# In the SSD scan of a two-block transformer kernel, GpSimd's row masks and the halving of the weight slabs change places

## The chip, the cores and the metric

The kernel runs on one core of one Trainium2 chip. The metric is device microseconds of one execution. Three runs of the kernel before gave 1665.68, 1666.03 and 1666.28 us, so the median is 1666.03 us.

## The reference, cut to what matters

The reference computes two residual blocks over 512 tokens of width 1024. The change lies in the second block's SSD mixer, a scan with 32 heads of 64 channels in 4 groups. For one head the reference computes, chunk by chunk,

```
a_cum    = cumsum(dt * A)
decay_in = exp(where(causal, a_cum[l] - a_cum[s], -inf))
y        = (C B^T * decay_in) (x * dt)           (+ the state carried from earlier chunks)
y        = (y + x * d_skip) * silu(z)
y        = rms_norm over each of the 4 groups of 512 channels
```

The kernel doesn't carry a state. It forms the whole causal 512 x 512 matrix of each head, of which 1280 columns per partition are kept (the causal blocks of 128 x 128), so the decay is one masked exponential of 128 x 1280 and the scan is one product of that matrix with the head's inputs.

## The kernel before, in words

Weights come as slabs of 1 MB (128 x 2048 f32). A slab is loaded by SyncE into one of three slots (`raw`). Then ScalarE writes its high half (`weight_head`, tile `w_hi`, line 458) and VectorE writes the rest (`weight_tail`, tile `w_lo`, line 994, `raw` minus `w_hi`). TensorE multiplies with both halves in three products (lines 1835 to 1837). `w_lo` has the same place as `raw`.

The stage of the change runs over 16 pairs of heads. Beside the pairs, TensorE makes the 16 tiles of z, two from each of 8 slabs. The slabs of the gates follow. Five engines work in a pipeline. Each engine runs its own list of instructions in order, and semaphores join the lists. I call one turn of the loop over `pair` a body, and name the instructions so:

- TensorE, body p: the tile z(p+1), then `pair_values(p)`, line 2292, which I call values(p). It needs both weighted rows of pair p and bank 6, which gated(p-1) sets free. After values(2), values(6) and values(10) the scores of the next group follow, line 2260.
- SyncE: `sum_row(hd)` loads the 128 x 1280 row of head hd from DRAM (line 387) into one of five buffers `p2`. The row of head hd may start when values((hd-5)//2) has ended.
- GpSimd: mask(hd) is `row_masked(hd)`, two affine selects of 128 x 256, lines 1788 and 1789. Body p runs mask(2p+4), product(p) (line 1799, y times the gate, which waits for gated(p)), mask(2p+5), square(p) (line 1802), and, except where p is a multiple of four, sum(p) (line 1805).
- ScalarE, body p: the tanh of z(p), then exp(2p+2) and exp(2p+3), four activations each, which wait for mask(2p+2) and mask(2p+3). Where p is odd, a `weight_head` follows.
- VectorE, body p: gated(p-1) (line 1456, which waits for values(p-1)), gate(p) (line 1450), where p is even and not zero a `weight_tail`, where p is 3, 7 or 11 the copies of a group's scores (line 1467), then weighted(2p+2) and weighted(2p+3) (line 1476), which wait for exp(2p+2) and exp(2p+3).

So gated(p) in VectorE's body p+1 releases product(p) on GpSimd, and weighted(2p+5) stands in that same body p+1, ahead of gated(p+1) in body p+2.

Of the kernel before, what the change touches and what calls it, by code (L numbers as in the profile page):

```python
# [28 lines left out]
SSD_H, SSD_P, SSD_G, XS_T, BC_T, TAPS = 32, 64, 4, 16, 8, 4  # L29
# [29 lines left out]
SLAB0, SLABS, FREED, PLACE, _freed, _freed_wide = {}, {}, {}, [], 0, 2  # L59
# [24 lines left out]
def build(nc, x_d, slabs_d, ada_d, cols_d, gate_w_d, pool_w_d, consts_d, inv_d, rope_d, qkg_d, out_d):  # L84
# [159 lines left out]
    def sem(name):  # L244
        if name not in sems:
            sems[name] = nc.alloc_semaphore(name)
        return sems[name]
# [29 lines left out]
    def paired(back):  # L277
        out, used = [], 0
        for j in (1, 0, 2, 3) if back else (0, 1, 3, 2):
            lo, hi = (0, P * (j + 1)) if back else (P * j, S)  # L280
            out.append((j, lo, hi, used))
            used += hi - lo
        return out
# [4 lines left out]
    def diagonals(a, back):  # L288

        first, wide = (P, a[:, 2 * P:]) if back else (7 * P, a[:, 0:8 * P])  # L290
        wide = wide.rearrange("p (r c) -> p r c", r=2)
        near = a[:, first:first + 2 * P].rearrange("p (r c) -> p r c", r=2)
        far = wide[:, :, 3 * P:] if back else wide[:, :, 0:P]
        return far, near
# [7 lines left out]
    def group_total(g):  # L302
        return xbc[:, XS_T + g, :]

    def group_square(pair):
        return xbc[:, XS_T + (SSD_G if pair % 4 else 0) + pair // 4, :]
# [62 lines left out]
    def width(n):  # L369
        return UQ_COLS if n in UQ_AT else SLAB  # L370

    block = nc.Block()
    with block:
# [79 lines left out]
        def _(act):  # L453
# [3 lines left out]
            def fn(out, in_, f, **kw):  # L457
                return act.activation(out, in_, f, **kw)  # L458
# [8 lines left out]
            def weight_head(n):  # L467

                act.wait_ge(sem(f"raw_in{n % SLOTS}"), 16 * (n // SLOTS) + 16)
                if n >= SLOTS:  # L470

                    act.wait_ge(sem("tile_done"), 2 * (n - SLOTS) + 2)
                do.tell(fn(w_hi[:, n % SLOTS, 0:width(n)], raw[:, n % SLOTS, 0:width(n)], ACT.Copy), "w_head", n + 1)
# [323 lines left out]
            def half_tanh(pair):  # L797
                act.wait_ge(sem("tile_done"), 2 * SLAB0["z"] + pair + 1)
                if pair >= 2:

                    act.wait_ge(sem("z_used"), pair - 1)
                do.tell(fn(zt[pair % 2][:], z_banks[pair % 2][:], ACT.Tanh, scale=0.5), "z_tanh", pair + 1)

            def exponentials(hd):
                act.wait_ge(sem("row_masked"), hd + 1)
                e2, shift = p2[hd % len(p2)], nac_col[:, :, hd:hd + 1]
                for j, lo, hi, used in paired(0):
                    row = e2[:, used:used + hi - lo]
                    ins = fn(row, row, ACT.Exp, bias=shift[:, j, :])
                    if j != TOK - 2:  # L810
                        do(ins)
                    else:
                        do.tell(ins, "e2_made", hd + 1)
# [3 lines left out]
            for pair in range(XS_T):  # L817
                half_tanh(pair)
                if pair + 1 < XS_T:
                    for hd in (2 * pair + 2, 2 * pair + 3):  # L820
                        exponentials(hd)
                if pair % 2:
                    weight_head(SLAB0["z"] + pair // 2 + 2)

            def group_root(g):
                act.wait_ge(sem("group_mean"), g + 1)
                do.tell(fn(rs_g[:, g, :], group_banks[g][:], ACT.Sqrt, bias=eps), "group_root", g + 1)
# [103 lines left out]
            for step in range(QH + 1):  # L931
                if step < QH:
                    hd = step
# [8 lines left out]
                if step:  # L942
                    hd = step - 1
# [39 lines left out]
        def _(dve):  # L983
# [6 lines left out]
            def weight_tail(n):  # L990

                dve.wait_ge(sem("w_head"), n + 1)
                part = slice(0, width(n))
                do.tell(dve.tensor_tensor(w_lo[:, n % SLOTS, part], raw[:, n % SLOTS, part], w_hi[:, n % SLOTS, part].bitcast(f32),  # L994
                                          ALU.subtract), "w_split", n + 1)
# [452 lines left out]
            def gate(pair):  # L1448
                dve.wait_ge(sem("z_tanh"), pair + 1)
                free(dve.scalar_tensor_tensor(zt[pair % 2][:], zt[pair % 2][:], 1.0, z_banks[pair % 2][:], ALU.add, ALU.mult), "z", pair)  # L1450

            def gated_pair(pair):

                y = xbc[:, pair, :]
                dve.wait_ge(sem("pv2_done"), TOK * (pair + 1))
                do.tell(dve.scalar_tensor_tensor(y, y, col("d_skip", pair), banks[6][:], ALU.mult, ALU.add), "ys_made", pair + 1)
# [5 lines left out]
            def scores_copied(g):  # L1462

                for j, lo, hi, used in sorted(paired(0), key=lambda block_row: block_row[0] != 2):
                    bank, first = score_place(j)
                    dve.wait_ge(sem("s2_done"), 2 * g + (1 if j == 2 else 2))
                    ins = dve.tensor_copy(sm[:, used:used + hi - lo], banks[bank][:, first:first + hi - lo])
                    if j >= 2:
                        do.tell(ins, "s2_taken", 2 * g + j - 1)
                    else:  # L1470
                        do(ins)

            def weighted_scores(hd):
                e2 = p2[hd % len(p2)]
                dve.wait_ge(sem("e2_made"), hd + 1)
                do.tell(dve.tensor_tensor(e2[:], e2[:], sm[:], ALU.mult), "p2_made", hd + 1)  # L1476
# [6 lines left out]
            for pair in range(XS_T):  # L1483
                if pair:
                    gated_pair(pair - 1)
                gate(pair)
                if pair % 2 == 0 and pair:
                    weight_tail(SLAB0["z"] + pair // 2 + 1)
                if pair % 4 == 3 and pair + 1 < XS_T:
                    scores_copied(pair // 4 + 1)  # L1490
                if pair + 1 < XS_T:
                    weighted_scores(2 * pair + 2)
                    weighted_scores(2 * pair + 3)
            gated_pair(XS_T - 1)
            weight_tail(SLAB0["gates"] + 1)
            dve.wait_ge(sem("z_used"), XS_T)
            for g in range(SSD_G):
                if g == SSD_G - 1:
# [229 lines left out]
        def _(pool):  # L1728
# [55 lines left out]
            def row_masked(hd):  # L1784

                pool.wait_ge(sem(f"row_in{hd % len(p2)}"), 16 * (hd // len(p2)) + 16)
                wide, near = diagonals(p2[hd % len(p2)], 0)
                do(pool.affine_select(wide, wide, [[0, 2], [1, P]], ALU.is_ge, never, base=0, channel_multiplier=-1))  # L1788
                do.tell(pool.affine_select(near, near, [[0, 2], [1, P]], ALU.is_ge, never, base=0, channel_multiplier=-1),  # L1789
                        "row_masked", hd + 1)  # L1790

            for hd in range(4):
                row_masked(hd)
            for pair in range(XS_T):
                if pair + 2 < XS_T:
                    row_masked(2 * pair + 4)

                pool.wait_ge(sem("ys_made"), pair + 1)
                do.tell(pool.tensor_tensor(xbc[:, pair, :], zt[pair % 2][:], xbc[:, pair, :], ALU.mult), "z_used", pair + 1)  # L1799
                if pair + 2 < XS_T:  # L1800
                    row_masked(2 * pair + 5)
                do(pool.tensor_tensor(group_square(pair), xbc[:, pair, :], xbc[:, pair, :], ALU.mult))
                if pair % 4:
                    total = group_total(pair // 4)
                    do.tell(pool.tensor_tensor(total, total, group_square(pair), ALU.add), "square_added", pair - pair // 4)

            for n in range(8, 16):
                pool.wait_ge(sem("key_scale"), n - 7)
# [6 lines left out]
            for hd in range(QH):  # L1815
# [5 lines left out]
                if hd >= 3 and hd % 2:  # L1821
                    pair = (hd - 3) // 2
# [797 lines left out]
```

## Time and profile before

| | |
|---|---|
| median of three runs | 1666.03 us |
| profiled execution: its own time, its span | 1667.77 us, 1666.0 us |
| TensorE busy with matmuls in the span | 98% (1635.8 us) |
| VectorE, ScalarE, GpSimd busy | 66%, 44%, 16% |
| mean granted TensorE clock | 0.999 |
| product (line 1799), 16 times | 1.284 us median, 3.226 us longest |
| ScalarE waiting for GpSimd's masks, 783 to 925 us | 38.9 us in 18 waits |
| VectorE waiting for ScalarE's exponentials, 783 to 925 us | 31.3 us in 13 waits |

Times in the tables and rows are microseconds from the span's start unless marked ns. Busy time counts the instruction from its start to its end, so an instruction that has been started and is held back counts as busy too. TensorE's matmuls are pipelined and their ends are modelled.

### The profile page before, as it was taken

What the parts mean: (1) busy time and instruction counts of PE and PEld (TensorE: products, weight loads), DVE (VectorE), ACT (ScalarE), POOL (GpSimd) and SP (SyncE); (2) the same over time, 40 slices, a digit from 0 to 9 for tenths busy, and PEclk for the clock granted to TensorE, in tenths of its full rate; (3) what the DMA queues carried; (4) which work ended last, traced back from release to release, by engine and by line L of the source; (5) the groups of instructions that cost most, each with busy time, mean ns of one, the idle gap of its engine ahead of it and who ended that gap; (6) DMA issues with size and microseconds to landing.
All of it is one profiled execution on the core that took longest, in us unless ns stands there. A gap on an engine that the chain in (4) does not pass through costs nothing.

```text
span 1666.0 us, 20328 instructions
## 1 busy us (share of the span) xinstructions
PE 1635.8 (98%) x7871; PEld 1313.4 (79%) x7871; DVE 1098.8 (66%) x1378; ACT 736.6 (44%) x971; POOL 258.5 (16%) x243
## 2 busy tenths in 40 slices
PE   6999999999999999999999999999999999999999
PEld 3888778888898887887666788886688888888887
DVE  2888878544575576877777865548868886642464
ACT  3443334222374236546676433538822454531241
POOL 0005100050220000001899200004600000000000
PEclk9999999999999999999999999999999999999999
DMA  9544322222222232225555222220032222222222
GB/s 386 200 186 177 142 77 101 83 95 102 101 102 101 99 129 82 100 78 201 196 204 182 76 101 74 95 101 26 2 114 89 101 102 101 86 91 101 101 101 101
DMA packets 30224, 195.33 MB, mean 117 GB/s; under 512 B 3376, under 2 KB 3856, under 8 KB 9904
## 3 DMA queue, kind: packets, MB, share of 16 engines
q1 hardware_dynamic: 26240, 167.66, 27.9%
q10 hardware_dynamic: 3888, 26.38, 4.0%
q8 instruction: 62, 1.02, 0.2%
q14 instruction: 34, 0.28, 0.1%
HBM read 189.66 MB, written 4.36 MB: 116 GB/s over the span
## 4 chain that ended last, share of the span: by engine, by line
PE 82%; DVE 7%; ACT 4%; POOL 4%; issue 1%; DMA 1%; ACTq 0%; SPq 0%; DVEq 0%; POOLq 0%
PE bank L1835 25%; PE bank L1837 24%; PE bank L1836 24%; DVE p L1476 2%; ACT p L458 2%; POOL p L1788 1%; PE bank L2408 1%; PE bank L2434 1%; PE bank L2420 1%; DMA x<-x_in 1%; POOL p L1789 1%; DVE w_lo L994 1%; PE bank L2125 1%; PE bank L2107 1%; POOL xbc L1799 1%
## 5 line engine op out<-in xcount | busy, mean ns | idle before, releaser
L1835 PE MATMUL bank<-h,w_hi 128*128 128x512 f32 (+1 forms) x1152 | 451.0, 392 | 3.7 <-DVE w_lo L994 3.0
L1836 PE MATMUL bank<-h,w_hi 128*128 128x512 f32 (+1 forms) x1152 | 445.1, 386 | 0.0
L1837 PE MATMUL bank<-h,w_lo 128*128 128x512 f32 (+1 forms) x1152 | 445.0, 386 | 0.0
L458 ACT ACTIVATE w_hi<-raw 128x2048 fp32r<-128x2048 f32 (+1 forms) x133 | 247.4, 1860 | 310.7 <-DMA raw<-slabs 301.6
L994 DVE TENSOR_TENSOR w_lo<-raw,w_hi 128x2048 fp32r<-128x2048 f32 (+1 forms) x125 | 291.5, 2332 | 98.2 <-ACT w_hi L458 94.8
L1835 PEld LDWEIGHTS bank<-h,w_hi 128*128 128x128 f32 x1152 | 216.4, 188 | 53.4 <-issue 5.6
L1837 PEld LDWEIGHTS bank<-h,w_lo 128*128 128x128 f32 x1152 | 216.4, 188 | 44.3
L1836 PEld LDWEIGHTS bank<-h,w_hi 128*128 128x128 f32 x1152 | 216.5, 188 | 43.7 <-issue 1.4
L1835 PE MATMUL bank<-a_hi,w_hi 128*128 128x512 f32 x432 | 168.3, 390 | 0.6 <-DVE a_lo L998 0.3
L1837 PE MATMUL bank<-a_hi,w_lo 128*128 128x512 f32 x432 | 168.1, 389 | 0.0
L1836 PE MATMUL bank<-a_lo,w_hi 128*128 128x512 f32 x432 | 168.1, 389 | 0.0
L1835 PEld LDWEIGHTS bank<-a_hi,w_hi 128*128 128x128 f32 x432 | 81.1, 188 | 18.0 <-DVE a_lo L998 0.7
L1836 PEld LDWEIGHTS bank<-a_lo,w_hi 128*128 128x128 f32 x432 | 81.1, 188 | 16.9
L1837 PEld LDWEIGHTS bank<-a_hi,w_lo 128*128 128x128 f32 x432 | 81.1, 188 | 16.9
L458 ACT ACTIVATE p<-p,nac_col 128x512 f32<-128x512 f32 (+3 forms) x128 | 72.1, 563 | 42.8 <-POOL p L1789 38.9
L1708 DVE SCALAR_TENSOR_TENSOR facc<-fpad,cols,facc 128x512 f32<-128x512 f32 x88 | 66.2, 752 | 32.6 <-ACT facc L458 30.2
L1088 DVE SCALAR_TENSOR_TENSOR x<-bank,mod,x 128x512 f32<-128x512 f32 x24 | 18.0, 751 | 99.0 <-PE bank L1837 98.9
L1476 DVE TENSOR_TENSOR p<-p,sm 128x1280 f32<-128x1280 f32 x32 | 56.0, 1749 | 32.3 <-ACT p L458 31.3
L1431 DVE SCALAR_TENSOR_TENSOR cacc<-cpad,cols,cacc 128x512 f32<-128x512 f32 x72 | 54.4, 755 | 29.2 <-ACT cacc L458 27.1
L1788 POOL TENSOR_SCALAR_AFFINE_SELECT p<-p 128x256 f32<-128x256 f32 x32 | 43.7, 1365 | 160.0 <-DMA p<-sum_rows 157.9
L1086 DVE TENSOR_TENSOR x<-bank,x 128x512 f32<-128x512 f32 x16 | 11.1, 692 | 69.4 <-PE bank L1837 69.4
L1835 PE MATMUL bank<-ys_hi,w_hi 128*128 128x512 f32 x128 | 50.6, 395 | 0.0
(403 smaller groups left out, 2523.4 us busy)
## 6 DMA issues: line engine op xcount, KB each, us to landing
raw<-slabs SPq DMA_DIRECT2D x127, 1024.0 KB, 4.8
ada_chunk<-ada ACTq DMA_DIRECT2D x24, 1024.0 KB, 7.0
p<-sum_rows SPq DMA_DIRECT2D x32, 640.0 KB, 5.5
x<-x_in SPq DMA_DIRECT2D x4, 1024.0 KB, 9.3
spill_x<-x SPq DMA_DIRECT2D x1, 2048.0 KB, 10.6
x<-spill_x SPq DMA_DIRECT2D x2, 1024.0 KB, 6.0
out<-x SPq DMA_DIRECT2D x8, 256.0 KB, 2.0
raw<-slabs SPq DMA_DIRECT2D x2, 768.0 KB, 4.2
```

Of the source, the lines that this page charges most:

```text
L458: return act.activation(out, in_, f, **kw)
L994: do.tell(dve.tensor_tensor(w_lo[:, n % SLOTS, part], raw[:, n % SLOTS, part], w_hi[:, n % SLOTS, part].bitcast(f32), ALU.subtract), "w_sp ...
L1088: ins = dve.scalar_tensor_tensor(x[:, m, :], bank[:], mod[:, gate + m:gate + m + 1], x[:, m, :], ALU.mult, ALU.add)
L1431: ins = dve.scalar_tensor_tensor(acc, pad[:, tap:tap + S], col("conv_w", TAPS * n + tap), acc, ALU.mult, ALU.add)
L1476: do.tell(dve.tensor_tensor(e2[:], e2[:], sm[:], ALU.mult), "p2_made", hd + 1)
L1708: ins = dve.scalar_tensor_tensor(acc, pad[:, tap:tap + S], col("convf_w", TAPS_F * tile + tap), acc, ALU.mult, ALU.add)
L1788: do(pool.affine_select(wide, wide, [[0, 2], [1, P]], ALU.is_ge, never, base=0, channel_multiplier=-1))
L1789: do.tell(pool.affine_select(near, near, [[0, 2], [1, P]], ALU.is_ge, never, base=0, channel_multiplier=-1), "row_masked", hd + 1)
L1799: do.tell(pool.tensor_tensor(xbc[:, pair, :], zt[pair % 2][:], xbc[:, pair, :], ALU.mult), "z_used", pair + 1)
L1835: pe.matmul(out, w[0], a[0], start=start, stop=False)
L1836: pe.matmul(out, w[0], a[1], start=False, stop=False)
L1837: return pe.matmul(out, w[1], a[0], start=False, stop=stop)
```

## The change

Three engines' lists change their order. No instruction is added or taken away, and no shape changes. On ScalarE the `weight_head` of a slab moves from the end of an odd body to the middle of the even body in front of it, between the two exponentials. On VectorE the `weight_tail` moves from the start of an even body to the middle of the odd body in front of it, between the two weighted rows. On GpSimd mask(2p+5) moves from between product and square to behind square and sum. The following mask(2p+6), which stood right behind the sum as the first of the next body, stays behind it.

```diff
             for pair in range(XS_T):
                 half_tanh(pair)
                 if pair + 1 < XS_T:
-                    for hd in (2 * pair + 2, 2 * pair + 3):
-                        exponentials(hd)
-                if pair % 2:
+                    exponentials(2 * pair + 2)
+                if pair % 2 == 0:
                     weight_head(SLAB0["z"] + pair // 2 + 2)
+                if pair + 1 < XS_T:
+                    exponentials(2 * pair + 3)
```

```diff
                 if pair:
                     gated_pair(pair - 1)
                 gate(pair)
-                if pair % 2 == 0 and pair:
-                    weight_tail(SLAB0["z"] + pair // 2 + 1)
                 if pair % 4 == 3 and pair + 1 < XS_T:
                     scores_copied(pair // 4 + 1)
                 if pair + 1 < XS_T:
                     weighted_scores(2 * pair + 2)
+                if pair % 2:
+                    weight_tail(SLAB0["z"] + pair // 2 + 2)
+                if pair + 1 < XS_T:
                     weighted_scores(2 * pair + 3)
             gated_pair(XS_T - 1)
-            weight_tail(SLAB0["gates"] + 1)
```

```diff
-            for hd in range(4):
+            for hd in range(5):
                 row_masked(hd)
             for pair in range(XS_T):
-                if pair + 2 < XS_T:
-                    row_masked(2 * pair + 4)
 
                 pool.wait_ge(sem("ys_made"), pair + 1)
                 do.tell(pool.tensor_tensor(xbc[:, pair, :], zt[pair % 2][:], xbc[:, pair, :], ALU.mult), "z_used", pair + 1)
-                if pair + 2 < XS_T:
-                    row_masked(2 * pair + 5)
                 do(pool.tensor_tensor(group_square(pair), xbc[:, pair, :], xbc[:, pair, :], ALU.mult))
                 if pair % 4:
                     total = group_total(pair // 4)
                     do.tell(pool.tensor_tensor(total, total, group_square(pair), ALU.add), "square_added", pair - pair // 4)
+                for hd in (2 * pair + 5, 2 * pair + 6):
+                    if hd < SSD_H:
+                        row_masked(hd)
```

## Rows read from the trace of the kernel before

**Rows 1.** One window of four bodies; columns: length, each engine's busy us, clock, DMA.
```profile
855.00:891.00 36.00, 34.25 (x172) 23.22 (x170) 27.59 (x23) 24.31 (x39) 33.08 (x28) 1.00 0.58 205
```
**Rows 2.** Waits of TensorE from 783 to 925 us: total, times, longest.
```profile
PE bank L2292 <- DVE xbc L1456: 4.2, 4, 1.1
PE bank L1835 <- DVE w_lo L994: 2.8, 4, 0.9
```
**Rows 3.** The chain that ended last, in order of time: start, us, what.
```profile
841.08 0.73 ACT p L458
...
848.66 2.01 DVE p L1476
850.75 2.44 DVE p L1476
```
**Rows 4.** Timeline of VectorE: start, us, line, operation, idle before and its releaser.
```profile
846.56 2.07 DVE L1467 COPY sm<-bank 128x256 f32<-128x256 f32 x4
...
853.22 0.75 DVE L1456 SCALAR_TENSOR_TENSOR xbc<-xbc,cols,bank 128x512 f32<-128x512 f32 x1
854.00 0.69 DVE L1450 SCALAR_TENSOR_TENSOR zt<-zt,bank 128x512 f32<-128x512 f32 x1
854.72 2.82 DVE L994 TENSOR_TENSOR w_lo<-raw,w_hi 128x2048 fp32r<-128x2048 f32 x1
857.58 1.57 DVE L1476 TENSOR_TENSOR p<-p,sm 128x1280 f32<-128x1280 f32 x1
861.97 1.49 DVE L1476 TENSOR_TENSOR p<-p,sm 128x1280 f32<-128x1280 f32 x1 [2.82 <-ACT p L458]
...
932.36 2.29 DVE L994 TENSOR_TENSOR w_lo<-raw,w_hi 128x2048 fp32r<-128x2048 f32 x1
```
**Rows 5.** Timeline of GpSimd over the same body.
```profile
849.41 2.42 POOL L1805 TENSOR_TENSOR xbc<-xbc 128x512 f32<-128x512 f32 x1
...
854.11 1.28 POOL L1799 TENSOR_TENSOR xbc<-zt,xbc 128x512 f32<-128x512 f32 x1 [0.19 <-DVE xbc L1456]
855.47 2.34 POOL L1788 TENSOR_SCALAR_AFFINE_SELECT p<-p 128x256 f32<-128x256 f32 x1
857.88 1.54 POOL L1789 TENSOR_SCALAR_AFFINE_SELECT p<-p 128x256 f32<-128x256 f32 x1
859.50 1.04 POOL L1802 TENSOR_TENSOR xbc<-xbc 128x512 f32<-128x512 f32 x1
860.62 1.29 POOL L1805 TENSOR_TENSOR xbc<-xbc 128x512 f32<-128x512 f32 x1
...
863.79 0.41 POOL L1789 TENSOR_SCALAR_AFFINE_SELECT p<-p 128x256 f32<-128x256 f32 x1
```
**Rows 6.** Timeline of ScalarE: the first body, then the body shown above.
```profile
784.09 4.73 ACT L458 ACTIVATE p<-p,nac_col 128x512 f32<-128x512 f32 x8 [1.35 <-POOL p L1789]
...
859.51 2.35 ACT L458 ACTIVATE p<-p,nac_col 128x512 f32<-128x512 f32 x4 [3.15 <-POOL p L1789]
861.90 0.60 ACT L458 ACTIVATE zt<-bank 128x512 f32<-128x512 f32 x1
...
869.11 1.93 ACT L458 ACTIVATE w_hi<-raw 128x2048 fp32r<-128x2048 f32 x1
```
**Rows 7.** Timeline of VectorE: gated(0) and gated(14).
```profile
790.45 0.75 DVE L1456 SCALAR_TENSOR_TENSOR xbc<-xbc,cols,bank 128x512 f32<-128x512 f32 x1
...
917.00 0.75 DVE L1456 SCALAR_TENSOR_TENSOR xbc<-xbc,cols,bank 128x512 f32<-128x512 f32 x1
```
**Rows 8.** Timeline of TensorE: one values(p).
```profile
864.39 2.37 PE L2292 MATMUL bank<-p,xdt 128*64 128x512 f32 x16 [1.02 <-DVE xbc L1456]
```
**Rows 9.** DMAs of the tile sum_rows, 36 issues: us from issue to landing.
```profile
DMA to landing us min/median/max: 3.7/5.4/7.7
```
**Rows 10.** Two windows around the one fall of TensorE's clock near 1142 us.
```profile
1136.00:1138.00 2.00, 0.88 (x8) 0.91 (x9) 1.36 (x6) 1.92 (x4) 1.33 (x3) 1.00 0.89 373
...
1143.00:1144.00 1.00, 1.00 (x2) 0.23 (x1) 0.68 (x2) 0.71 (x3) 0.91 (x2) 0.50 0.00 0
```

## The prediction

> **What bounds the kernel now.** I read the window sums first. TensorE is busy 98% of the span, but over four bodies of the SSD loop, 36.00 us, it is busy 34.25 us while GpSimd counts 33.08 [rows 1]. The waits of TensorE come next: in the loop it stands 4.2 us for gated(p) and 2.8 us for `w_lo` [rows 2], 7.0 us in all. The chain in order of time then shows whose chain it is: it runs through GpSimd's mask, ScalarE's exponential, VectorE's weighted rows and gated(p) [rows 3], and comes back to GpSimd.
>
> The timelines give the cycle. gated(7) starts at 853.22, product(7) at 854.11, and mask(19) is through at 859.42. The exponential starts at 859.51, weighted(19) at 861.97, and gated(8) at 863.49 (861.97 + 1.49 + 0.03) [rows 4 to 6]. Body 8 thus takes 10.27 us. From gated(0) to gated(14) there are 14 bodies in 917.00 - 790.45 = 126.55 us [rows 7], 9.04 each. TensorE alone needs about 33 to 34 us for four. So the stage has two bounds close to each other, and a longer cycle shows in the time at once.
>
> **What one port does.** Two engines hold each other back. The `weight_tail` issued at 854.72 takes 2.82 us where one alone takes 2.29 [rows 4]: it begins its work at 857.54 - 2.29 = 855.25, 0.14 before product(7) ends (855.39). A weighted row takes 1.49 alone and 2.44 behind a sum that ends at 851.83: again it begins 0.14 to 0.15 before that end [rows 3, 5]. The other way round, the sum issued at 849.41 ends 1.16 after the weighted row in front (850.67), its own 1.29 less 0.13. A select of 0.41 ends 0.27 after the VectorE instruction that it met: 857.81 behind the tail's 857.54, and 859.42 behind the weighted row's 859.15 [rows 4, 5]. gated and gate keep 0.75 and 0.69 beside GpSimd's work, so these two are taken as free of it.
>
> The Trainium skill, "SBUF — State Buffer", section "SBUF: two separate sides", describes this as an exclusive lock on a shared port pair: a VectorE instruction with two SBUF inputs and a GpSimd instruction take turns, and the loser blocks fully. The trace agrees (2.82 against 2.29). By the page the sum comes out as it does below; with no lock it would be 1671 in place of 1701.
>
> **Part 1: mask(2p+5) behind square and sum.** This is the step that costs. It stands on the cycle gated(p), product(p), mask(2p+5), exp(2p+5), weighted(2p+5), gated(p+1). The change puts square(p), 1.04, and sum(p), 1.29, each with a gap of 0.07 to 0.08, between product and mask, onto the cycle. mask(2p+6) is needed one body later and doesn't gain anything that was missing.
>
> I work out one body from the start of gated (0.00), all with the durations above.
> - Without any lock: product 0.89 to 2.18, square 2.25 to 3.29, sum 3.37 to 4.66, two selects to 5.62, exponential 5.71 to 8.07, weighted row 8.18 to 9.67, gated 9.70. Without a sum 8.33. Both are lower bounds of a body.
> - With the lock, even bodies (sum, no tail). exp(2p+2) is early: exp(2p+1) ended 0.11 before weighted(2p+1), that is at -1.63, and a tanh of 0.60, an exponential of 2.35 and gaps bring it to 1.39 [rows 6]. So weighted(2p+2) is issued at 1.50, held by product to 2.03, ends 3.52. Square, issued 2.25, ends at 3.52 + 0.91 = 4.43, sum at 5.79, the selects at 6.28 and 6.76. Exponential 6.85 to 9.21, weighted 9.32 to 10.81, gated at 10.84.
> - Bodies 1, 5, 9, 13 (no sum, but the moved tail). As above to square 4.43. The tail is issued at 3.55, held by square to 4.28, ends 6.57. The first select waits for it: 6.85. The second 7.33. Exponential 7.42 to 9.78, weighted 9.89 to 11.38, gated at 11.41.
> - Bodies 3, 7, 11 (copies, sum and tail). The copies take 1.50 to 3.57 [rows 4] and let square (3.29) pass. Sum 3.37 to 4.66 holds the weighted row, which ends at 6.00; the first select ends 6.28. The tail, issued 6.03, runs to 8.42; the second select ends 8.69. Exponential 8.78 to 11.14, weighted to 12.74, gated at 12.77.
>
> The 14 bodies are 7 x 10.84 + 4 x 11.41 + 3 x 12.77 = 75.9 + 45.6 + 38.3 = 159.8 us, against 126.55: **+33.3 us**.
>
> **Part 2: ScalarE's half earlier.** `weight_head` takes 1.93 [rows 6]. In body 0 the masks are long made and exp(2), exp(3) follow each other without a gap (4.73 for eight activations), so the head delays exp(3), weighted(3) and gated(0) by 1.93 + 0.03: **+1.95 us**. From body 2 on exp(2p+2) ends at 1.39 and mask(2p+3) at 6.76, so the head ends at 3.35 and is hidden by the wait for GpSimd; were that cover gone, it would cost 1.95 in every even body.
>
> **Part 3: VectorE's rest earlier.** TensorE needs the slab two bodies later, so its 2.8 us of waits for `w_lo` go. They buy nothing: TensorE's next wait, for gated, grows instead. The cost of the tail on the cycle is in part 1. After the loop one tail of 2.3 us less stands in VectorE's list, beside 16 tiles of gates that keep TensorE busy; I take 0.
>
> **Rows and slabs.** No DMA is added. Row 2p+5 starts when values(p) ends and lands in 5.4, at most 7.7 us [rows 9]. values(p) starts once gated(p-1) has ended, 0.87 after its start, takes 2.37 [rows 8], and the next gated(p) is 11 us after gated(p-1). So the row lands at most 3.24 + 7.7 = 10.9 after gated(p-1), about when gated(p) starts, and its mask is not due for 4.5 us more. SyncE's order of rows and slabs stays, and a slab waits for z tiles that TensorE ends earlier in its list than the values a row waits for. 0.
>
> **Sum.** +33.3 + 1.95 = +35.2 us. The profiled execution took 1667.77 for a span of 1666.0, so the span would be 1701.2 and its own time 1703.0. On the median of the runs, 1.7 lower: 1666.0 + 35.2 = **1701.2 us**.
>
> **The rivals.**
> - *The lock costs less than it seems.* Square then hides behind the weighted row, or the select gets in ahead of the tail. Without tails on the cycle: 4 x 9.45 + 10 x 10.84 = 146.2, +19.6 + 1.95, 1687.6 us. With no lock at all: 4 x 8.33 + 10 x 9.70 = 130.3, +3.8 + 1.95, 1671.7 us. For it: the lock's length after a select is read from two rows. Against: it repeats in every pair of instructions shown. 15%, nearly all of it at the upper price.
> - *TensorE's clock falls in the wider gaps.* TensorE has about 8 us of work in a body of 11.4, so it stands 3.5 us in each. Near 1142 the clock was at its lower level, 1.2 GHz (0.50), after TensorE had stood still and then run matmuls with breaks; at 1136 to 1138, with 0.88 us busy of 2.00, it was still 1.00 [rows 10]. A body wholly at 1.2 GHz is 2 x 7.9 = 15.8 us, so it decides only where most of a body runs so; a short fall costs less than the 3.5 us that TensorE waits. With half of the 14 bodies at the lower level: 7 x (15.8 - 11.4) = +31 more, 1732 us; with three of them, 1714. 8%. The Trainium skill, "TensorE: Matmul & The Clock Gate", section "What's actually happening", says that an idle TensorE is put to half its clock. No run here shows such gaps repeated.
> - *The other side: TensorE is the bound afterwards.* Its two waits of 7.0 us go and the time is 1666.0 - 7.0 = 1659 us. It needs the cycle to be under 8.5 us, so mask(2p+5) must be off it: GpSimd would have to take it while product or square waits. For it: GpSimd's selects lose up to 1.93 us each to the tail in bodies of 10.27, and the tail moves. Against: its list is in order, and the cycle without any lock is already 9.70. It decides once GpSimd's part, 5.62 us from gated to the last select without any lock, falls under 4.4. 3%, with results down to no change put here.
>
> **How the numbers follow.** Forecast 74%, less lock 15%, clock 8%, other side 3%. The forecast's own spread is some 4 us either way (0.3 us in each of 14 bodies). The range reaches to the first rival's upper price and the smaller clock case: 1686 to 1714. A difference of 0.2% is 3.3 us, about what can be told from no change: faster 2%, same 2%, slower 96%.
>
> **What would show it.** Right: in GpSimd's timeline the selects follow the sum; from gated to gated 10.8, 11.4 and 12.8 us in that pattern; no wait for `w_lo`, 30 to 40 us of TensorE's waits for gated; ScalarE's waits for masks near 5 us in even bodies; weighted rows of 2.0 us beside product. Gated(0) comes 2 us late. Wrong: selects of 0.41 throughout (no lock), a granted clock below 0.95 in the loop, GpSimd waiting for rows, or bodies under 9 us.

## The result and the profile after

The changed kernel takes 1701.13 us, the median of 4 runs (1700.54 to 1702.94), against 1665.86 us of the kernel before. The ratio is 1.0214, with a 95% interval of 1.0196 to 1.0231. It is slower by 35.3 us; 35.2 us were forecast. The profiled execution took 1702.94 us for a span of 1701.2 us. Its line numbers are shifted: gated is L1457, gate L1451, a weighted row L1477, a `weight_tail` L995, product L1798, square L1799, sum L1802, the two selects of a mask L1789 and L1790.

First the waits from 783 to 962 us (total, times, longest), one line each for TensorE, VectorE, ScalarE and GpSimd:

```profile
PE bank L2292 <- DVE xbc L1457: 31.0, 11, 4.7
...
DVE p L1477 <- ACT p L458: 65.4, 16, 5.8
...
ACT p L458 <- POOL p L1790: 70.7, 14, 7.4
...
POOL xbc L1798 <- DVE xbc L1457: 63.8, 15, 6.6
```

The wait for `w_lo` is gone, as the change means it to be, and TensorE's wait for gated has grown from 4.2 to 31.0 us [rows 2]. VectorE, ScalarE and GpSimd wait for each other in a ring: GpSimd for gated, ScalarE for the mask, VectorE for the exponential. TensorE stands outside and waits for the ring. No engine is the bound; the way round is.

The timeline of VectorE shows bodies 7, 8 and 9, from gated to gated:

```profile
859.45 0.75 DVE L1457 SCALAR_TENSOR_TENSOR xbc<-xbc,cols,bank 128x512 f32<-128x512 f32 x1
860.23 0.69 DVE L1451 SCALAR_TENSOR_TENSOR zt<-zt,bank 128x512 f32<-128x512 f32 x1
860.95 2.07 DVE L1468 COPY sm<-bank 128x256 f32<-128x256 f32 x4
863.06 2.40 DVE L1477 TENSOR_TENSOR p<-p,sm 128x1280 f32<-128x1280 f32 x1
865.49 2.38 DVE L995 TENSOR_TENSOR w_lo<-raw,w_hi 128x2048 fp32r<-128x2048 f32 x1
870.67 1.49 DVE L1477 TENSOR_TENSOR p<-p,sm 128x1280 f32<-128x1280 f32 x1 [2.80 <-ACT p L458]
872.20 0.75 DVE L1457 SCALAR_TENSOR_TENSOR xbc<-xbc,cols,bank 128x512 f32<-128x512 f32 x1
...
873.70 2.02 DVE L1477 TENSOR_TENSOR p<-p,sm 128x1280 f32<-128x1280 f32 x1
881.47 1.49 DVE L1477 TENSOR_TENSOR p<-p,sm 128x1280 f32<-128x1280 f32 x1 [5.75 <-ACT p L458]
883.00 0.75 DVE L1457 SCALAR_TENSOR_TENSOR xbc<-xbc,cols,bank 128x512 f32<-128x512 f32 x1
...
886.55 3.02 DVE L995 TENSOR_TENSOR w_lo<-raw,w_hi 128x2048 fp32r<-128x2048 f32 x1
892.85 1.49 DVE L1477 TENSOR_TENSOR p<-p,sm 128x1280 f32<-128x1280 f32 x1 [3.28 <-ACT p L458]
894.38 0.75 DVE L1457 SCALAR_TENSOR_TENSOR xbc<-xbc,cols,bank 128x512 f32<-128x512 f32 x1
```

They take 12.75, 10.80 and 11.38 us; 12.77, 10.84 and 11.41 were worked out. Body 8 of before took 10.27 [rows 4]. The timeline of GpSimd in body 8 shows the new order on the way:

```profile
873.10 1.27 POOL L1798 TENSOR_TENSOR xbc<-zt,xbc 128x512 f32<-128x512 f32 x1 [4.01 <-DVE xbc L1457]
874.45 2.17 POOL L1799 TENSOR_TENSOR xbc<-xbc 128x512 f32<-128x512 f32 x1
876.69 1.27 POOL L1802 TENSOR_TENSOR xbc<-xbc 128x512 f32<-128x512 f32 x1
878.04 0.41 POOL L1789 TENSOR_SCALAR_AFFINE_SELECT p<-p 128x256 f32<-128x256 f32 x1
878.52 0.41 POOL L1790 TENSOR_SCALAR_AFFINE_SELECT p<-p 128x256 f32<-128x256 f32 x1
```

Square takes 2.17 in place of 1.04 because it met the weighted row of 873.70, and that row takes 2.02 in place of 1.49 because it met product. Between product and mask there are now 3.7 us (878.04 - 874.37) where there was a gap of 0.08 [rows 5]. ScalarE's exponential starts at 879.02, right behind the select of 878.52.

### The profile page after: what moved, and what is told of

Its sections match the earlier page's. It is cut to its first block, busy times and chain, and to the rows that moved or that the text cites. A ratio compares the mean times of both kernels' runs of the same rounds, so it can differ in the third digit from the quotient of the medians.

```text
span 1701.2 us, 20328 instructions
## 1 busy us (share of the span) xinstructions
PE 1647.2 (97%) x7871; PEld 1319.4 (78%) x7871; DVE 1099.5 (65%) x1378; ACT 736.1 (43%) x971; POOL 243.0 (14%) x243
## 4 chain that ended last, share of the span: by engine, by line
PE 81%; DVE 6%; POOL 5%; ACT 5%; issue 1%; DMA 1%; ACTq 0%; SPq 0%; POOLq 0%; DVEq 0%
PE bank L1835 24%; PE bank L1837 24%; PE bank L1836 24%; ACT p L458 3%; PE bank L2408 2%; POOL xbc L1799 2%; DVE p L1477 1%; PE bank L2434 1%; PE bank L2420 1%; POOL xbc L1798 1%; POOL p L1789 1%; DMA x<-x_in 1%; DVE w_lo L995 1%; PE bank L2125 1%; PE bank L2107 1%
## 5 line engine op out<-in xcount | busy, mean ns | idle before, releaser
L995 DVE TENSOR_TENSOR w_lo<-raw,w_hi 128x2048 fp32r<-128x2048 f32 (+1 forms) x125 | 292.2, 2337 | 100.5 <-ACT w_hi L458 97.1
L1477 DVE TENSOR_TENSOR p<-p,sm 128x1280 f32<-128x1280 f32 x32 | 56.0, 1749 | 66.3 <-ACT p L458 65.4
L2292 PE MATMUL bank<-p,xdt 128*64 128x512 f32 (+3 forms) x256 | 46.7, 516 | 31.0 <-DVE xbc L1457 31.0
L2292 PEld LDWEIGHTS bank<-p,xdt 128*64 128x64 f32 x256 | 20.5, 159 | 54.9 <-DVE p L1477 35.4
```

The lines of the kernel that those rows point to most:

```text
L2292: last = pe.matmul(banks[6][64 * half:64 * half + 64, lo:hi], xdt[:, j, SSD_P * hd:SSD_P * hd + SSD_P], p2[hd % len(p2)][:, used:used + hi ...
```

## The experiments

Each experiment is compared with runs of the kernel before on the same chip (median 1666.43 us for the first four, 1666.23 us for the last two). Its line numbers can differ by a few from those above, so the rows are told apart by their operations and tiles.

**e1_masks_only.** GpSimd's part alone.

```diff
-            for hd in range(4):
+            for hd in range(5):
                 row_masked(hd)
             for pair in range(XS_T):
-                if pair + 2 < XS_T:
-                    row_masked(2 * pair + 4)
...
-                if pair + 2 < XS_T:
-                    row_masked(2 * pair + 5)
...
+                for hd in (2 * pair + 5, 2 * pair + 6):
+                    if hd < SSD_H:
+                        row_masked(hd)
```

> GpSimd's part of the change alone; ScalarE's and VectorE's lists stay as before. Theory A (mask(2p+5) behind square and sum stands on the cycle gated, product, mask, exponential, weighted row, gated): the tail now stands at the start of the even bodies, so the bodies take about 12.8, 10.8, 12.8 and 9.5 us in place of 10.8, 12.8, 10.8 and 11.4, and their sum is the same as with the whole change: +33 us, 1699 us. Theory B (the slab halves in the middle of the bodies cost the time, GpSimd's order is harmless): no more than 2 us over the kernel before, 1668 us.

Measured: 1701.26 us, ratio 1.0209 (1.0194 to 1.0224). The bodies from gated(4) on take 9.44, 12.76, 10.84 and 12.74 us, and the 14 bodies 159.6 us, against 159.4 with the whole change. The next rows are VectorE's timeline of this kernel in body 5, with no tail in it (gated 835.99 to 845.43):

```profile
835.99 0.75 DVE L1456 SCALAR_TENSOR_TENSOR xbc<-xbc,cols,bank 128x512 f32<-128x512 f32 x1
...
843.91 1.49 DVE L1476 TENSOR_TENSOR p<-p,sm 128x1280 f32<-128x1280 f32 x1 [4.41 <-ACT p L458]
845.43 0.75 DVE L1456 SCALAR_TENSOR_TENSOR xbc<-xbc,cols,bank 128x512 f32<-128x512 f32 x1
```

So the order of GpSimd's list costs the whole 35 us by itself (1701.26 - 1666.43 = 34.8). Where the tail stands changes which body is long, and not the sum. Theory B falls.

**e2_halves_only.** ScalarE's and VectorE's part alone, GpSimd as before.

```diff
+                    exponentials(2 * pair + 2)
+                if pair % 2 == 0:
                     weight_head(SLAB0["z"] + pair // 2 + 2)
+                if pair + 1 < XS_T:
+                    exponentials(2 * pair + 3)
...
                     weighted_scores(2 * pair + 2)
+                if pair % 2:
+                    weight_tail(SLAB0["z"] + pair // 2 + 2)
+                if pair + 1 < XS_T:
                     weighted_scores(2 * pair + 3)
```

> ScalarE's and VectorE's part alone; GpSimd's list stays as before. Theory A: weighted(2p+3) now stands behind a tail, and the tail meets GpSimd's second mask in odd bodies; bodies of about 10.3, 8.4, 10.6 and 8.7 us, so +5 to +6 us, 1671 to 1672 us, and TensorE's waits for w_lo are gone. Theory B: +33 us, 1699 us. A third theory, that the earlier halves are good in themselves and only GpSimd's part spoils them: 1666 less TensorE's 2.8 us of waits for w_lo, 1663 us.

Measured: 1671.85 us, ratio 1.0030 (1.0019 to 1.0041), +5.4 us. The bodies from gated(2) on take 10.57, 8.63, 9.18 and 8.62 us. Its waits of TensorE in the loop:

```profile
PE bank L2293 <- DVE xbc L1457: 10.5, 11, 1.9
```

The 2.8 us for `w_lo` are gone, and the waits for gated grow by more than that, from 4.2 to 10.5 us. The earlier halves lose by themselves too, so the third theory falls with theory B. Beside the masks' move they cost nothing that can be measured, since 1701.13 and 1701.26 us are the same: the costs of two edits on one ring don't add.

**e3_masks_first.** The kernel before, with the mask moved the other way.

```diff
                 if pair + 2 < XS_T:
                     row_masked(2 * pair + 4)
+                    row_masked(2 * pair + 5)
...
-                if pair + 2 < XS_T:
-                    row_masked(2 * pair + 5)
                 do(pool.tensor_tensor(group_square(pair), xbc[:, pair, :], xbc[:, pair, :], ALU.mult))
```

> The kernel before, but GpSimd takes mask(2p+5) before product(p), right behind mask(2p+4); the halves stay as before. Theory A: the mask leaves the cycle through product(p); it then waits only for its row, which may start when values(p) has ended and lands 5 to 8 us later. With 5.5 us to land the bodies average 8.9 us: 1664 us, between 1662 and 1670 with the landing time. If the mask were not what sets the cycle (rival: the port's lock alone does, wherever the mask stands), the time would stay at 1666 or rise, since the same instructions still meet.

Measured: 1662.71 us, ratio 0.9977 (0.9967 to 0.9986). It beats both kernels, by 3.7 us the one before. The 14 bodies take 123.1 us (913.97 - 790.87) against 126.6. The window of [rows 1], then TensorE's waits in the loop:

```profile
855.00:891.00 36.00, 35.55 (x182) 23.83 (x178) 31.64 (x23) 25.55 (x41) 34.00 (x28) 1.00 0.61 209
```
```profile
PE bank L1834 <- DVE w_lo L994: 1.5, 1, 1.5
PE bank L2291 <- DVE xbc L1456: 0.9, 2, 0.5
```

TensorE is busy 35.55 of 36.00 us (34.25 before [rows 1]) and waits 2.4 us in the loop, not 7.0. GpSimd's timeline shows the meetings with VectorE still there, but behind the masks, where they hold no exponential back (product is L1800 here, square L1801, sum L1804):

```profile
853.51 0.41 POOL L1788 TENSOR_SCALAR_AFFINE_SELECT p<-p 128x256 f32<-128x256 f32 x1
853.99 0.41 POOL L1789 TENSOR_SCALAR_AFFINE_SELECT p<-p 128x256 f32<-128x256 f32 x1
854.49 3.21 POOL L1800 TENSOR_TENSOR xbc<-zt,xbc 128x512 f32<-128x512 f32 x1
857.77 2.17 POOL L1801 TENSOR_TENSOR xbc<-xbc 128x512 f32<-128x512 f32 x1
860.02 2.42 POOL L1804 TENSOR_TENSOR xbc<-xbc 128x512 f32<-128x512 f32 x1
```

Product takes 3.21 us here, and no mask of the same turn stands behind it. The rival, that the lock costs the same wherever the mask stands, falls.

**e4_short_squares.** The whole change with short squares and sums; three quarters of the group sums are left out.

```diff
-                do(pool.tensor_tensor(group_square(pair), xbc[:, pair, :], xbc[:, pair, :], ALU.mult))
+                do(pool.tensor_tensor(group_square(pair)[:, 0:P], xbc[:, pair, 0:P], xbc[:, pair, 0:P], ALU.mult))
...
-                    do.tell(pool.tensor_tensor(total, total, group_square(pair), ALU.add), "square_added", pair - pair // 4)
+                    do.tell(pool.tensor_tensor(total[:, 0:P], total[:, 0:P], group_square(pair)[:, 0:P], ALU.add), "square_added", pair - pair // 4)
```

> The whole change, but square(p) and sum(p) run over 128 of 512 columns (three quarters of the group sums are left out). It tells the order from the lock. Theory A with the lock: weighted rows and tails still hold square and the selects; bodies of about 9.3, 9.5, 9.6 and 10.7 us: +12 us, 1678 us. Order without a lock: the cycle falls to 9.7 - 1.6 = 8.1 us, under TensorE's 8.5, and the time to 1660 us. If square and sum are not on the cycle at all: 1701 us as with the change.

Measured: 1679.68 us, ratio 1.0077 (1.0060 to 1.0094). The bodies from gated(4) on take 10.75, 9.35, 9.63 and 9.35 us. GpSimd's timeline has a square of a quarter's length twice, and VectorE's shows what stood beside it:

```profile
844.39 1.53 POOL L1799 TENSOR_TENSOR xbc<-xbc 128x128 f32<-128x128 f32 x1
...
853.75 0.40 POOL L1799 TENSOR_TENSOR xbc<-xbc 128x128 f32<-128x128 f32 x1
```
```profile
843.64 2.02 DVE L1477 TENSOR_TENSOR p<-p,sm 128x1280 f32<-128x1280 f32 x1
...
852.99 2.07 DVE L1468 COPY sm<-bank 128x256 f32<-128x256 f32 x4
```

The first met a weighted row (843.64, 2.02 us) and took 1.53 us; the second met a copy out of PSUM and took 0.40. So order and lock both count. For an order without a lock 1660 us was worked out, and for square and sum off the ring 1701; the measured time is at neither. No run takes the lock itself away: it is shown by the lengths of the instructions that meet, and by bodies that come out as worked out with it.

**e5_mask_between.** The whole change, with mask(2p+5) between square and sum.

```diff
+                if 2 * pair + 5 < SSD_H:
+                    row_masked(2 * pair + 5)
                 if pair % 4:
...
-                for hd in (2 * pair + 5, 2 * pair + 6):
-                    if hd < SSD_H:
-                        row_masked(hd)
+                if 2 * pair + 6 < SSD_H:
+                    row_masked(2 * pair + 6)
```

> The whole change, but mask(2p+5) stands between square(p) and sum(p), so only square lies between product and the mask. Theory A: every body with a sum loses about the sum's 1.29 + 0.07 us, more where the port comes free sooner: bodies of about 11.4, 9.5, 10.1 and 9.6 us, 17 to 18 us over the kernel before, 1684 us. If instead the two masks standing together, or the halves in the middle of the bodies, set the time, it stays at 1700 us.

Measured: 1684.45 us, ratio 1.0108 (1.0091 to 1.0124). The bodies from gated(4) on take 11.38, 9.44, 10.07 and 9.57 us. GpSimd's timeline shows the mask between square and sum (L1804) in a body of 9.44 us, and VectorE's the gated at both its ends:

```profile
846.61 2.17 POOL L1799 TENSOR_TENSOR xbc<-xbc 128x512 f32<-128x512 f32 x1
848.85 0.41 POOL L1789 TENSOR_SCALAR_AFFINE_SELECT p<-p 128x256 f32<-128x256 f32 x1
849.32 0.41 POOL L1790 TENSOR_SCALAR_AFFINE_SELECT p<-p 128x256 f32<-128x256 f32 x1
849.81 1.27 POOL L1804 TENSOR_TENSOR xbc<-xbc 128x512 f32<-128x512 f32 x1
```
```profile
844.36 0.75 DVE L1457 SCALAR_TENSOR_TENSOR xbc<-xbc,cols,bank 128x512 f32<-128x512 f32 x1
...
853.80 0.75 DVE L1457 SCALAR_TENSOR_TENSOR xbc<-xbc,cols,bank 128x512 f32<-128x512 f32 x1
```

The sum alone costs 16.7 us of the 35 (1701.13 - 1684.45), in 10 of the 14 bodies: 1.2 to 1.4 us in those without copies, 2.7 us in the three with copies, where it also made the weighted row and the tail late.

**e6_masks_first_halves.** The order of e3_masks_first, with the earlier halves of the change (the diff of e2_halves_only beside this one).

```diff
                     row_masked(2 * pair + 4)
+                    row_masked(2 * pair + 5)
```

> GpSimd takes mask(2p+4) and mask(2p+5) before product(p), as in e3_masks_first, and now ScalarE's and VectorE's lists are those of the change. By the durations of the rows the tail between the two weighted rows holds gated back in odd bodies (10.0 us in bodies 3, 7, 11), so it is 2 to 3 us slower than with the halves in their old place: 1665 to 1667 us. Rival: with the masks early the earlier w_lo removes TensorE's last waits for it (1.5 us there), and it is the fastest of all: 1661 us.

Measured: 1665.36 us, ratio 0.9993 (0.9983 to 1.0002): no difference from the kernel before, and 2.7 us more than e3 by the medians. All ten runs (1664.05 to 1666.55) lie above all ten of e3 (1662.07 to 1663.93), but the two ran on different chips, and the intervals of their ratios touch. So the halves are likely better where they were; the rival of 1661 us falls. In the profiled execution TensorE waits 3.4 us for gated in the loop, in six waits, and the 14 bodies add up to 121.6 us, less than in e3. The traces can't show where the 2.7 us are: the profiled execution here is the fastest of its ten and that of e3 the second slowest of its ten, with spans of 1662.3 and 1662.1 us. That stays open.

## Why the prediction was right, point by point

- **The bound.** The ring through GpSimd's mask was named from the chain and the return of gated, and e1 and e3 show it from both sides: a mask later costs 35 us, a mask earlier gives 3.7.
- **Part 1, +33.3 us.** The 14 bodies took 950.91 - 791.55 = 159.36 us, so +32.8. Each kind of body came within 0.05 us. The term of lock and order holds: e4 shortens what stands ahead of the mask, e5 takes the sum from there, and both land within 2 us of the 1678 and 1684 worked out with the lock.
- **Part 2, +1.95 us, mis-sized.** gated(0) came 1.10 us later, not 1.95, and 0.49 of that is the work before it, which ran later in this execution (its first exponentials start at 777.86, not 777.37). The prediction said that in body 0 the masks are long made. The row it named showed a wait of 1.35 us for one [rows 6], which I passed over. In the changed kernel the first select ran before it met VectorE, and ScalarE had no such wait, as the timelines of GpSimd and ScalarE show:

```profile
780.79 0.41 POOL L1789 TENSOR_SCALAR_AFFINE_SELECT p<-p 128x256 f32<-128x256 f32 x1 [21.57 <-DMA p<-sum_rows]
```
```profile
783.25 2.35 ACT L458 ACTIVATE p<-p,nac_col 128x512 f32<-128x512 f32 x4
785.63 1.91 ACT L458 ACTIVATE w_hi<-raw 128x2048 fp32r<-128x2048 f32 x1
787.57 2.35 ACT L458 ACTIVATE p<-p,nac_col 128x512 f32<-128x512 f32 x4
```

  The price of the head itself was right. From the first exponentials to gated(0) it is 13.69 us here (791.55 - 777.86) and 11.76 in e1_masks_only (790.16 - 778.40), which has no head there and no such wait either: 1.93 us. The kernel before took 13.08 in its profiled execution (790.45 - 777.37), with the wait. So the prediction had the head right and the kernel before wrong: in the execution profiled, ScalarE waited in that place already.
- **Part 3, 0.** Right: the waits for `w_lo` went and bought nothing. e2 shows the waits for gated grown to 10.5 us in their place.
- **The clock, taken as a rival and not as a term.** The clock did fall, at values(4), (6), (8), (10), (12) and (15), for part of a body each time. These are TensorE's timeline at values(6) and a window beside it:

```profile
849.54 3.71 PE L2292 MATMUL bank<-p,xdt 128*64 128x512 f32 x16 [3.29 <-DVE xbc L1457]
```
```profile
851.00:853.00 2.00, 2.00 (x12) 1.02 (x8) 1.18 (x1) 0.97 (x1) 2.00 (x1) 0.50 0.00 0
```

  values(6) takes 3.71 us in place of 2.37, at 0.50 of the clock (1.2 GHz). In the loop this is hidden. The next values starts late for it, without a wait:

```profile
861.30 2.37 PE L2292 MATMUL bank<-p,xdt 128*64 128x512 f32 x16
```

  That is 1.1 us after gated(6) ended (860.20), but gated(7), which needs the result, stands behind a weighted row until 872.20. The bodies show it too: bodies 2 and 3, around values(2) at the full clock, take 10.79 and 12.75 us, and bodies 6 and 7, around values(6), 10.80 and 12.75. TensorE's spare time was smaller than the rival's text had it: 31.0 us of waits in 14 bodies are 2.2 us each, not 3.5, and a fall uses up part of it. The fall isn't hidden at the end, where TensorE is the bound again:

```profile
951.81 3.58 PE L2292 MATMUL bank<-p,xdt 128*64 128x512 f32 x16 [2.78 <-DVE xbc L1457]
955.32 3.28 PE L2315 MATMUL bank<-xbc,mean 128*128 128x512 f32 x6
```

  values(15) takes 1.2 us more than at the full clock, and the prediction had nothing for that. values(15) started 33.9 us late (951.81 against 917.89), and the span is 35.2 us longer. So the three terms were +1.1, +32.8 and, unforeseen, about +1.3. That the sum of 35.2 us is closer than its parts is luck: small errors of both signs met.
- **The signs.** The pattern of the bodies, the 31.0 us of waits and the rows of 2.02 us came as named. Two did not: ScalarE's wait for the mask in body 8 (before its exponential of 879.02) is 3.50 us, not near 5, as the prediction's own working gives (6.85 - 3.35), and gated(0) is 1.1 us late, not 2. And one sign of being wrong did appear: a granted clock below 0.95 in the loop, 0.93 in this row of windows (length, each engine's busy us, clock, DMA):

```profile
848.00:894.00 46.00, 37.52 (x168) 25.23 (x168) 27.80 (x23) 24.49 (x39) 27.99 (x27) 0.93 0.46 161
```

  So the clock rival was right that the clock falls in such a loop, and wrong in the price: it needed most of a body at the lower level, and the falls were shorter.
- **The rivals.** Less lock: out, by the square of 2.17 us and the bodies of e4. TensorE as the bound afterwards: out here, but e3 is the order that does it, and 1662.7 us is near the 1659 worked out for that case. GpSimd never waited for a row in the loop of the changed kernel; in e3, where its masks come one step earlier, it waited for rows twice (8.3 us together, 6.6 of them in one wait).

## What to carry to other kernels

In a ring of engines, look for the instruction that hands on to the next engine, and put in front of it only what that next engine needs. Work that is off the ring, like the squares here, stands best behind the hand-over (e3 is the fastest kernel of all). Ahead of it, it costs its length (the sum 1.2 to 1.4 us a body), plus what it meets and holds back on VectorE (2.7 us in the bodies with copies). A wait that a change removes (2.8 us here) is worth nothing while the ring is longer than the engine that waited.

## What the runs showed of the hardware that was not expected

TensorE's clock fell to 1.2 GHz in a loop in which TensorE waits 2.8 to 4.7 us for gated in eight of 14 bodies and at most 1.2 us in the others. Six of the eight long waits went with a fall. The length of the wait alone doesn't tell which: it fell after a wait of 2.78 us at values(15), and stayed at 1.00 after 3.07 us at values(2) and 3.34 us at values(14). Over 848 to 894 us the mean granted clock was 0.93, and it was back at 1.00 within a body each time. In e2_halves_only, whose waits for gated add up to 10.5 us, the mean over the whole run stayed at 1.000; with the whole change it was 0.992.

The lock between VectorE and GpSimd depends on the partner. The same square of 128 x 128 took 0.40 us beside a copy out of PSUM and 1.53 us beside a product of two SBUF tiles, and the copies, gate and gated kept 2.07, 0.69 and 0.75 us beside GpSimd's work in every row shown here.
